# A two-direction state recurrence: transposes first in a step, score products between levels four and five, running sums in two buffers, and the first chunk's keys prepared ahead of its rows

## The reference

```python
def wkv_scan(state0, r, decay, kk, b, v, k, reverse):
    def step(S, inp):
        r_t, w_t, kk_t, b_t, v_t, k_t = inp
        sa = jnp.einsum("bhvk,bhk->bhv", S, kk_t)
        S = (S * w_t[:, :, None, :] - sa[..., None] * b_t[:, :, None, :]
             + v_t[..., None] * k_t[:, :, None, :])
        return S, jnp.einsum("bhvk,bhk->bhv", S, r_t)
    ...
    S, ys = lax.scan(step, state0, xs, reverse=reverse)

for d in range(N_DIR):                       # N_DIR = 2: forward and backward in time
    decay = jnp.exp(-DECAY_SCALE * jax.nn.sigmoid(lp["w0"][d] + jnp.tanh(w_lo) @ lp["w_up"][d]))
    a = jax.nn.sigmoid(lp["a0"][d] + a_lo @ lp["a_up"][d])
    k_d = k * (1 + (a - 1) * lp["k_a"])
    state, y = wkv_scan(init[d], rh, to_heads(decay), kk, kk * to_heads(a), vh, to_heads(k_d),
                        reverse=(d == 1))
```

## Time and profile before

| | us |
|---|---|
| median of 3 runs (1621.16 to 1626.23) | 1623.47 |
| the profiled execution's own time | 1618.29 |
| its span, first to last instruction | 1616.3 |
| prologue of the loop, gates ready to first scores | 249 to 272 |
| step loop, n = -2 to 11 | 272 to 547 |

### The profile page before, as it was taken

One profiled execution on the slowest core, in us unless ns is written; L12 is line 12 of the kernel. 1 busy time (PEld: TensorE's weight loads), 2 busy tenths in 40 slices (PEclk: granted clock), 3 DMA queues, 4 the chain that ended last, 5 costly groups with the idle time before them and its releaser, 6 DMA issues.

```text
span 1616.3 us, 34976 instructions
## 1 busy us (share of the span) xinstructions
PE 1502.0 (93%) x14628; PEld 1241.5 (77%) x14628; DVE 906.0 (56%) x1471; ACT 600.3 (37%) x1042; POOL 257.2 (16%) x280
## 2 busy tenths in 40 slices
PE   5899996999999988999999998999879999999997
PEld 3687873888888776877877886877758788888885
DVE  1624215676677738888885225777454655565222
ACT  3422344334543434344343223545644332223221
POOL 0000003455444010111110211000001111111111
PEclk9999997899999999999999998999889999999998
DMA  8242100333210222232222321212002222222321
GB/s 349 78 149 80 53 27 1 107 108 95 82 42 4 80 79 75 81 104 80 101 96 90 108 97 64 99 54 79 27 29 103 84 98 104 99 82 98 106 90 70
DMA packets 38745, 139.64 MB, mean 86 GB/s; under 512 B 3040, under 2 KB 3552, under 8 KB 38112
## 3 DMA queue, kind: packets, MB, share of 16 engines
q1 hardware_dynamic: 38480, 135.76, 24.3%
q10 hardware_dynamic: 144, 2.10, 0.4%
HBM read 135.75 MB, written 2.10 MB: 85 GB/s over the span
## 4 chain that ended last, share of the span: by engine, by line
PE 64%; DVE 13%; ACT 3%; issue 3%; POOL 0%; DVEq 0%; ACTq 0%; POOLq 0%
PE bank L681 45%; PE bank L818 7%; DVE ffn_sb L2573 5%; PE bank L690 2%; DVE arena L2342 1%; DVE w_up L2172 1%; PE bank L627 1%; PE bank L1328 1%; PE bank L891 1%; PE bank L936 1%; ACT w_up L1446 1%; PE bank L902 1%; ACT arena L1818 1%; PE bank L915 1%; PE bank L917 1%
## 5 line engine op out<-in xcount | busy, mean ns | idle before, releaser
L681 PE MATMUL bank<-hf_hi,w_up 128*128 128x512 f32 x1376 | 424.0, 389 | 0.0
L681 PEld LDWEIGHTS bank<-hf_hi,w_up 128*128 128x128 f32 x1376 | 258.3, 188 | 53.2
L681 PE MATMUL bank<-hf_lo,w_up 128*128 128x512 f32 x688 | 269.5, 392 | 8.0 <-DVE w_up L2172 8.0
L681 PE MATMUL bank<-act_hi,w_down 128*128 128x512 f32 x704 | 216.6, 389 | 0.0
L1446 ACT ACTIVATE w_up<-ring 128x1024 fp32r<-128x1024 f32 x88 | 93.0, 1058 | 216.2 <-PE bank L681 216.2
L818 PE MATMUL bank<-arena 64*64 64x32 f32 (+1 forms) x4224 | 153.3, 226 | 14.7 <-DVE arena L2299 9.4
L2172 DVE TENSOR_TENSOR w_up<-ring,w_up 128x1024 fp32r<-128x1024 f32 x88 | 108.1, 1229 | 104.4 <-ACT w_up L1446 104.3
L818 PEld LDWEIGHTS bank<-arena 64*64 64x64 f32 x4224 | 143.1, 142 | 25.2 <-DVE arena L2299 11.4
L681 PEld LDWEIGHTS bank<-hf_lo,w_up 128*128 128x128 f32 x688 | 129.1, 188 | 40.8 <-DVE w_up L2172 13.3
L2573 DVE SCALAR_TENSOR_TENSOR ffn_sb<-ffn_sb 128x512 f32<-128x512 f32 x176 | 151.5, 861 | 5.5
L681 PEld LDWEIGHTS bank<-act_hi,w_down 128*128 128x128 f32 x704 | 132.2, 188 | 27.3
(11 more groups left out here) (326 smaller groups left out, 2360.7 us busy)
## 6 DMA issues: line engine op xcount, KB each, us to landing
ring<-w SPq DMA_DIRECT2D x76, 1024.0 KB, 4.9
ring<-w SPq DMA_DIRECT2D x32, 704.0 KB, 4.0
ring<-w SPq DMA_DIRECT2D x64, 256.0 KB, 2.9
arena<-w SPq DMA_DIRECT2D x2, 3072.0 KB, 22.8
x<-xT SPq DMA_DIRECT2D x1, 2048.0 KB, 12.0
arena<-w SPq DMA_DIRECT2D x2, 1024.0 KB, 19.2
x<-xT ACTq DMA_DIRECT2D x1, 2048.0 KB, 8.0
outT<-x SPq DMA_DIRECT2D x4, 512.0 KB, 2.7
```

The costliest lines, as they stand in the source:

```text
L681: ins = mm(out, w[:, a, k, :], of_block(b, k0 + k), start=first and k == 0 and m == 0, stop=last and k == n - 1 and m == 2)
```

## The change

- **PE.** `turned(m, d)` goes to the very start of a step (it stood between `nx` and `dx` of level 3). The score products of direction 0 go ahead of `nx` of level 5, those of direction 1 ahead of `dx` of level 5. Before the loop, `bonus_sum` goes ahead of `values_turned`.
- **DVE.** Running sums of chunk q + 1 are made in step n behind level 3; before, those of chunk q behind `w_out` of level 2. `scores_out(q, 0)` goes ahead of `w_out` of level 5, `first_level` and `first_turned` are parted by direction, and `y_last` goes ahead of direction 1's. Bonuses go ahead of values.
- **ACT.** `decay_exps` and `keys_in` of chunk q + 1 are the last work of step n.
- **GpSimd.** A direction's keys are made at once; for chunk 0 they come ahead of its rows.
- **Buffers.** `cum` gets a second buffer, `plast` a fourth place. The operand `gup` is loaded later, into a gate buffer that has come free, behind the paced weight loads of the SP queue. Products at the end wait by another semaphore.

```diff
@@ (scan buffers)
-                self.cum = rstd[:, NJ * L * d:NJ * L * d + NJ * L].rearrange("p (j t) -> p j t", j=NJ)
+                self.cum = [rstd[:, NJ * L * d:NJ * L * d + NJ * L].rearrange("p (j t) -> p j t", j=NJ), AS.take(NJ, L)]
@@ SP
-            sp.dma_start(gup_sb, gup).then_inc(s["lora_in"], 16)
...
+            sp.wait_ge(s["bh0"], 2 * NCC)
+            sp.dma_start(gup_sb, gup).then_inc(s["gup_in"], 16)
             load_stage("W_OUT", w8, 37, 2)
@@ PE, before the loop
-            for c in range(-1, NC):
-                values_turned(c)
             pe.wait_ge(s["rkr"], NJ)
             for j in range(NJ):
                 bonus_sum(j)
+            for c in range(-1, NC):
+                values_turned(c)
@@ PE, the loop
+                if 0 <= m < NC - 1:
+                    for d in both:
+                        turned(m, d)
                 if n >= 0:
                     for d in both:
                         state_in(n, d)
...
-                if 0 <= m < NC - 1:
-                    for d in both:
-                        turned(m, d)
                 if inv:
                     for d in both:
                         dx(m, d, 3)
...
-                    for d in both:
-                        nx(m, d, 5)
                 if prep:
                     scores(q, 0)
                 if inv:
                     for d in both:
-                        dx(m, d, 5)
+                        nx(m, d, 5)
                 if prep:
                     scores(q, 1)
                 if inv:
+                    for d in both:
+                        dx(m, d, 5)
@@ ACT, decay_exps and the loop
-                    done("S", d, q - 2)
+                    done("S", d, q - 3)
...
-                if q < NC:
-                    decay_exps(q)
...
+                if q + 1 < NC:
+                    decay_exps(q + 1)
+                    keys_in(q + 1)
@@ POOL, before the loop
             undecayed(0)
-            pool.wait_ge(s["pre_out"], 2 * NJ + NC + 1)
+            steps.last()
+            keys_decayed(0, 0)
+            pool.wait_ge(s["pre_out"], 2 * NJ)
+            keys_decayed(0, 1)
+            rows_decayed(0, 1)
+            pool.wait_ge(s["pre_mm"], 2 * NJ + NC + 1)
+            rows_decayed(0, 0)
+            undecayed(1)
@@ DVE, the loop
-                if 0 < q < NC:
-                    for d in both:
-                        running_sums(q, d)
...
+                if q + 1 < NC:
+                    for d in both:
+                        running_sums(q + 1, d)
...
-                    for d in both:
-                        w_out(m, d, 5)
                 if prep:
                     scores_out(q, 0)
                 if inv:
                     for d in both:
+                        w_out(m, d, 5)
+                if prep:
+                    first_level(q, 0)
+                if inv:
+                    for d in both:
                         x_out(m, d, 5)
-                    for d in both:
                         x_turned(m, d, 5)
+                    w_out(m, 0, 6)
+                if prep:
+                    first_turned(q, 0)
+                if inv:
+                    w_out(m, 1, 6)
                 if prep:
                     scores_out(q, 1)
                 if inv:
                     for d in both:
-                        w_out(m, d, 6)
+                        y_last(m, d)
                 if prep:
-                    for d in both:
-                        first_level(q, d)
-                    for d in both:
-                        first_turned(q, d)
-                if inv:
-                    for d in both:
-                        y_last(m, d)
+                    first_level(q, 1)
+                    first_turned(q, 1)
```

More of the change, by code:

```diff
@@ L1654, in _ @@
             keys_in(0)
+            decay_exps(0)
             for n in range(-2, NC):
@@ L2286, in running_sums @@
             def running_sums(q, d):
[L2288 to L2290 removed]
+                done("bh", d, 2 * q - 2)
+                done("kh", d, 2 * q - 2)
+                to, gate = flat(scans[d].cum[q % 2]), flat(gates[:, d, 0, place(d, q) // L])
                 if d == 1:
@@ L2460, in _ @@
                 dve.wait_ge(s["y_root_mm"], j + 1)
-                dve.wait_ge(s["y_gated"], j + 1)
+                if j < 2:
+                    steps.last(1 - j)
                 steps.do(V.tensor_tensor(gate_gain[:, j, :], gate_gain[:, j, :], banks[4 + j][:, :], ALU.mult))
```

93 lines of the change are left out of this document (47 added, 46 removed).

## The result

The changed kernel takes 1630.3 us, the kernel before 1622.7 (medians of 20 runs each): ratio 1.0041, 95% interval 1.003 to 1.0052. The prediction, 1616.1 with a range to 1622, is 14 us too low and on the wrong side. The profiled execution took 1631.4 us against 1618.3.

A forecast was written before the change was run, and what follows sets the result against it. Bound taken: before the loop, a chain over DVE, POOL and PE; in the steps, PE and DVE by turns. Terms -6.9 + 0.3 + 1.3 + 0.2 - 2.3 = -7.4 us took 1623.5 to 1616.1, range 1608 to 1622.

The forecast's parts named there:

- Clock: Where the loop begins, PE regains two thirds of 3.4 us lost to the lower clock: -2.3, bounds 0 and -3.4.
- Prologue: Before the loop, reordered work lets level 2 begin at about 271.4 instead of 278.32: -6.9 us, bounds -5.4 and -7.7.
- Level 3: In each step, `dx` of level 3 starts earlier once the transposes leave: -0.45 us per step, not their 1.09.
- Running sums: Ahead of level 4's masks, the moved sums add +0.7 us per context step, n = 0 to 3; covered in token steps.
- Levels 4 to 6: From level 4's adds to the next level 2, a step takes 9.75 us instead of 9.45 to 9.6: +0.2 per step.
- Keys on time: Keys ready before level 4 save 0.9 us each in n = 7 to 9, 0.25 for n = 2 and 3: -3.2.
- POOL beside DVE: In the steps, POOL's products delay the pair of predicated copies on the path: 0.25 us, bounds 0 and 0.6.
- The slower one: Rival: DVE's long stretch grows in every step, slower by over 0.3% at 1.15 us each: 1629 us, chance 0.08.
- The rival in which the clock gives more: Rival: both lower-clock stretches near the loop's beginning go, gaining 1.1 and some 4 us more: 1611 us, chance 0.17.

The follow-up runs named there:

- turned back: The changed kernel with the keys turned at their old place again, between the two products of level 3: 1622.4 us, ratio 0.9990 to the kernel before.
- prologue alone: The kernel before with only the first chunk's part of the change (bonuses ahead of values, keys ahead of rows): 1615.5 us, ratio 0.9952.
- sums and scores back: The changed kernel with running sums behind the masks of level 2 again and the old order of the scores: 1625.6 us, ratio 1.0019.

## Why the prediction was wrong

**The step that failed is the term "Clock", -2.3.** I asked what the prologue would do to the granted clock and never what the moved work would do to it in the steps. The measured sign is the other: over the runs 0.0065 lower than before, worth about 7.7 us. Its part for the prologue was right in direction: with that part alone the clock rises by 0.0047 (the trace of that kernel has the loop 1.4 us shorter, 267.7 against 269.1). The fall from there, 0.011, comes with the edits of the loop. That transposes put into the hole at level 3 undo it is shown (10.4 us back, and 9.8 with both holes filled); that the idle time itself is the cause is the likeliest reading and not shown.

This term accounts for 10.0 of the 15.0 us by which the change was misjudged (+7.6 measured, -7.4 forecast). The other 5 (1 to 8 by the slopes of single kernels) lie in terms without clock; the place of the sums is the one that the runs point at, below.

**Prologue, -6.9: right in kind, somewhat small.** The trace shows -8.5, beyond the bound of -7.7: from first scores to level 2 it takes 4.2 us, at the higher clock, where I had 5.2. The kernel with this part alone is -8.0 in the median; that holds the clock too, so it stands against -6.9 and -2.3 together.

**Level 3, -0.45: right as counted, wrong in what it left out.** The stretch from level 2 to level 4 went from 12.94 to 12.45 us in n=4 to 6. I wrote that moving 1.09 us of transposes makes `dx` earlier by 0.45 only; the other half is the hole. I took it for lost time of no consequence, and with it went the clock: 14 us for the edit.

**Running sums, +0.7 in a context step: right beside the turned keys, too small without them.** In the changed kernel the stretch to the second direction's products of level 4 grew from 10.84 to 11.81, +1.0, a part of it at the lower clock; to the first direction's it is +0.64. Without the turned keys it is 12.7 against 11.05 to 11.8, since there the pair of scans lies beside POOL's keys; DVE's timeline of "turned back" has it at 1.75 us and not 1.25:

```profile
333.24 1.75 DVE L2311 TENSOR_TENSOR_SCAN rstd<-k_,arena 128x256 f32<-128x256 f32 x2
```

Four or five steps by 1.0 to 1.6 are 4 to 8 of the 13.9 us, where the sum had 3.0. The rest goes with the clock (0.0063, by the slope 7.6). Filling this hole gave only 3.8 back, so here the path counts at least as much as the clock.

**Levels 4 to 6, +0.2 per step: right at equal clock.** In n=5 level 2 of the next step starts 11.3 us behind the adds of level 4 (434.60 to 445.90), where I had 9.75. But 3.4 us of it are at the lower clock, which is 1.7 us of work: 9.6.

**Keys on time, -3.2: right in direction; its size is shown for one step.** The wait of the earlier trace rows is gone, and steps n=7 to 9 fall from 65.8 us (prologue alone: 21.96, 22.50, 21.34) to 61.7 with sums, turned keys and scores as before. A part of that is the clock (0.97, 0.92 and 1.00 against 1.00); n=9, at the full clock in both, gives 0.95, where I had 0.9.

**POOL beside DVE, 0.25: right in size.** The first pair of copies in n=5 took 1.20 us, predicted 0.88 alone and up to 1.5 (the pairs of n=-1 to 8 took 1.2 to 1.4):

```profile
437.62 1.20 DVE L2347 COPY_PREDICATED arena<-k_,arena 64x128 f32<-64x128 uint32 x2
```

**The rivals.** None had this mechanism. The slower one asked for steps longer by 1.15 us each through DVE's long stretch; that stretch did not grow. Its 0.08 was on the right side for a wrong reason. The rival in which the clock gives more was of the right kind and the wrong sign: I had noted that nothing around the stretch of PE busy for 10.21 of 10.24 us at the lower clock explained it, and then priced the clock as if it followed the prologue's idle time alone.

**What stays open.** How a hole of 0.46 us can lower the clock, and which holes and which fillings count. The old hole of 1.12 us had no effect, a new one of 0.46 had much, and own narrow products moved into it did nothing. The stretches at the lower clock do not follow the holes at a fixed distance (12 us in n=4), so no trace shows the link directly; it rests on the fillings. The short waits of levels 5 and 6 that the new score order brings (0.52 us in n=4) were not filled. With the hole filled, keys turned first still cost 9 us in the new score order, of which the clock explains none (0.9656 against 0.9633); the fillings' own time is part of that, in n=7 to 9 above all.

**The better kernel** is the change without the two moves: sums behind the masks of level 2, keys turned at level 3, all else kept. 1608.5 us, ratio 0.9921 (0.9894 to 0.9947), 0.8% under the kernel before and 22 us under the changed one.

## What to carry to other kernels

Price every move of TensorE work twice: by what waits for it, and by the hole that it leaves behind, since here the granted clock fell with a hole of half a microsecond in each step and made work far from it longer (eight transposes 1.81 us, not 1.09). Check such a theory by filling the hole with work without use, no longer than the hole; if the kernel gets faster, what the move took away was worth more than the work. It doesn't tell whether idle time or missing work was the reason: for that, fill with two kinds of work, and look where the idle time went. And read a step's time together with its granted clock, in the windows: PE busy for 95% of a stretch that has grown is no proof that there is more work.

## What the hardware showed that was not expected

- A single kernel's runs differ by up to 19 us (sums and scores back: 1616.6 at clock 0.964 to 1635.2 at 0.948), nearly all of it with the granted clock (correlation -0.98). One profiled execution of such a kernel says little on a change of 5 us.
- Adding 40 transposes took 10.4 us off a kernel (clock 0.9569 to 0.9682). The Trainium skill, "TensorE: Matmul & The Clock Gate", section "Part 4: PE-mode transpose", says that a transpose does not count as busy time in the same way. The run with the filling differs from it: here transposes brought the clock back. The same page, section "A second HAM failure mode: psum-queue depth-cycling", tells of short, frequent idle times between groups of products with which the clock swings between its two levels; the traces agree with it in that much, with a hole of 0.46 us in each step and a clock of 0.85 over four steps, 0.98 when it is filled.
- The clock was lower over stretches in which PE had no idle time at all, 10.24 of 10.24 us in the changed kernel as 10.21 of 10.24 before.
- DVE's pair of scans took 1.25 us alone and 1.75 beside POOL's products: not only copies are held up by them.
